# Turning round the gate/up product of the fuller expert of each pair in a one-core decoder step

## The reference, cut to what matters

```
D_MODEL, N_EXPERTS, TOP_K, EXPERT_DIM = 1024, 64, 8, 256
def one_block(args):
    tok_b, w_b, e = args
    xb = x_pad[tok_b]
    hb = jax.nn.silu(xb @ w_gate[e]) * (xb @ w_up[e])
    return (hb @ w_down[e]) * w_b[:, None]
...
return jax.ops.segment_sum(out.reshape(n_rows, d), tok_p, num_segments=t + 1)[:t]
```

## Time and profile before

| | |
|---|---|
| device time, median of three runs | 1811.39 us (1807.18 to 1811.45) |
| span of the profiled execution | 1803.0 us |
| before the expert stage (0 to 818.5 us) | 818.5 us |
| expert stage (818.5 to 1716 us) | 897.5 us, TensorE busy 893.16 us |
| after it (1716 to 1803 us) | 87.0 us |
| DMA share in the expert stage | 0.91 |

### The profile page before, as it was taken

How to read it: one execution, slowest core, us unless ns; L and a number is a source line. 1 busy time by engine, 2 the same in 40 slices (tenths; PEclk the granted TensorE clock), 3 DMA queues, 4 the chain that set the end, 5 groups by cost and what they waited for, 6 DMA issues and landing times.

```text
span 1803.0 us, 25610 instructions
## 1 busy us (share of the span) xinstructions
PE 1672.9 (93%) x8473; PEld 1204.3 (67%) x8474; DVE 1132.6 (63%) x1511; ACT 888.3 (49%) x1325; POOL 654.7 (36%) x555
## 2 busy tenths in 40 slices
PE   4999999589998898688999999999999999999997
PEld 3555555323356667366888888888888888888843
DVE  2355575541235556566777777777777777777746
ACT  1011111232336455136666776667676667676633
POOL 0056676300000000104555555555555555555410
PEclk8999999689999999789999999999999999999999
DMA  9688866677771113647998999989999989998874
GB/s 331 211 285 285 274 207 212 233 222 237 233 238 63 68 53 156 258 159 277 312 302 292 303 300 310 310 288 308 307 303 311 291 305 314 304 318 285 276 225 183
DMA packets 151909, 457.38 MB, mean 254 GB/s; under 512 B 29592, under 2 KB 39794, under 8 KB 126169
## 3 DMA queue, kind: packets, MB, share of 16 engines
q1 hardware_dynamic: 111097, 368.08, 55.7%
q0 software_dynamic: 30720, 69.83, 17.0%
q10 hardware_dynamic: 9960, 17.83, 2.9%
HBM read 403.40 MB, written 86.54 MB: 272 GB/s over the span
## 4 chain that ended last, share of the span: by engine, by line
PE 56%; DVE 2%; ACT 1%; issue 0%; DMA 0%; ACTq 0%; POOLq 0%; DVEq 0%
PE ps L2229 29%; PE ps L2246 15%; PE ps L2215 5%; PE ps L2534 2%; PE ps L2552 1%; PE ps L2253 1%; PE ps L1885 1%; PE ps L1856 1%; PE ps L1840 0%; DMA xg<-h_d,tokb 0%; DVE sums L1941 0%; DVE pairs L1908 0%; DVE gsc L1911 0%; ACT hT L2496 0%; DVE left L1931 0%
## 5 line engine op out<-in xcount | busy, mean ns | idle before, releaser
L2229 PE MATMUL ps<-hi_gu,xT_hi 128*128 128x512 f32 x768 | 309.5, 403 | 0.0
L2274 DVE TENSOR_TENSOR lo_gu<-raw_gu,hi_gu 128x1024 fp32r<-128x1024 f32 x256 | 304.3, 1221 | 4.5
L2229 PE MATMUL ps<-hi_gu,xT_lo 128*128 128x512 f32 x768 | 301.1, 392 | 0.0
L2229 PE MATMUL ps<-lo_gu,xT_hi 128*128 128x512 f32 x768 | 299.4, 390 | 0.0
L2168 ACT ACTIVATE hi_gu<-raw_gu 128x1024 fp32r<-128x1024 f32 x256 | 260.8, 1064 | 0.0
L2127 POOL DMA_INDIRECT acc_d<-yb,tokb x96 | 227.9, 2374 | 43.8 <-ACT yb L2182 24.9
L2108 POOL DMA_INDIRECT xg<-h_d,tokb x96 | 101.4, 1056 | 388.3 <-PE ps L2215 343.9
L602 PE MATMUL ps<-w_in_sb,hT 128*128 128x512 f32 x512 | 223.7, 594 | 1.1 <-ACT hT L466 1.1
L446 POOL TENSOR_TENSOR prod<-kring,qbc 128x512 f32<-128x512 f32 x128 | 158.8, 1270 | 177.1 <-DMA kring<-in_cache_k 119.2
L2182 ACT ACTIVATE yb<-ps,wslot 128x1024 f32<-128x1024 f32 x96 | 107.0, 1115 | 137.4 <-PE ps L2246 137.4
L602 PEld LDWEIGHTS ps<-w_in_sb,hT 128*128 128x128 f32 x512 | 95.9, 190 | 117.6 <-issue 116.3
(11 more groups left out here) (343 smaller groups left out, 2601.8 us busy)
## 6 DMA issues: line engine op xcount, KB each, us to landing
raw_gu<-in_expert_w_gate SPq DMA_DIRECT2D x64, 1024.0 KB, 8.6
raw_gu<-in_expert_w_up SPq DMA_DIRECT2D x64, 1024.0 KB, 12.1
raw_dn<-in_expert_w_down SPq DMA_DIRECT2D x64, 1024.0 KB, 7.6
kring<-in_cache_k SPq DMA_DIRECT2D x128, 256.0 KB, 3.2
vring<-in_cache_v SPq DMA_DIRECT2D x128, 256.0 KB, 3.1
adaw<-in_ada_w ACTq DMA_DIRECT2D x7, 2048.0 KB, 12.7
adaw<-in_ada_w SPq DMA_DIRECT2D x5, 2048.0 KB, 15.9
w_in_sb<-in_w_in SPq DMA_DIRECT2D x4, 2048.0 KB, 19.2
```

The costliest lines, as they stand in the source:

```text
L2229: last = pe.matmul(ps[:, 2 + b % 2, :].rearrange("p (a f) -> p a f", a=2), x[b % 2][:, k, :], w[:, :, k * F:(k + 1) * F], start=(k == 0 an ...
L2274: dve.tensor_tensor(lo_cut(n, u), raw_cut(n, u), hi_cut(n, u).bitcast(F32), ALU.subtract).then_inc(lo_made, 1)
```

## The change

The caps of the experts change. A table gives the heavy expert of pair p a cap of 224, 208, 192, 176 or 160 rows (4, 8, 8, 8 and 4 pairs; 192 on average) in place of 256; the light one stays at 128. With the counts above no expert is over its cap, before or after, so the overflow loop has no block in either.

For the heavy expert the operands of gate/up are turned round. The weights are stationary, 128 columns at a time, and the expert's transposed rows stream, all of them at once. They lie in `xT_h` as [chunk][hi | lo][cap], so that one matmul with w_hi streams both parts (2·cap columns: x_hi·w_hi into the first cap columns of a bank, x_lo·w_hi into the next), and a second one with w_lo streams x_hi (cap columns). The product is made in two halves of the hidden width, ch 0 and 1, each of 32 matmuls over both banks 2 and 3 (`gate_up_heavy`). Since the sum is in two halves of a bank, ScalarE copies the second half to SBUF (`second_halves`) and VectorE adds (`add_halves`) before silu. The hidden rows come out transposed, and the two blocks of the heavy expert need no `turn_h`. The down product of the light expert of the pair before stands between the two halves. The light expert is computed as before, from its own buffers, and its bank is one of the two.

The second block of a heavy expert gathers, evicts and scatters cap-128 rows in place of 128. The twelve cuts of a pair are spread over five places (`cuts_at`). The down weights are loaded with another split of the 256 hidden rows, so that a partition gets two pieces of 4 KB in place of one of 8 KB. The routing code computes the caps from the table.

```diff
+CAPS = [224] * 4 + [208] * 8 + [192] * 8 + [176] * 8 + [160] * 4 + [P] * PAIRS
...
-            w_from, = addressed(sp, ew_down[0][bass.ds(e, 1)].rearrange("o (p c) n -> p (o c n)", c=FC))
+            w_from, = addressed(sp, ew_down[0][bass.ds(e, 1)].rearrange("o (c p) n -> p (o c) n", p=P))
...
+                of = {HEAVY_FIRST: [(light, 0), (light, 1), (light, 2)],
+                      HEAVY_MID: [(light, 3), (heavy, 4)],
+                      HEAVY_LATE: [(heavy, 5), (light, 4)],
+                      LIGHT_FIRST: [(light, 5), (after, 0), (after, 1)],
+                      LIGHT_LATE: [(after, 2), (after, 3)]}[stage]
...
+            def second_halves(p, ch):
+                t, cap = 2 * p + ch, cap_of(2 * p)
+                act.wait_ge(gu_mm, turn_of(2 * p, ch))
...
+                act.activation(half2[:, :, 0:cap], ps[:, 2:4, cap:2 * cap], ACT.Copy).then_inc(half2_here, 1)
...
+            for p in range(PAIRS):
+                round_x(3 * p + 2)
+                round_weights(cuts_at(p, HEAVY_FIRST))
+                second_halves(p, 0)
+                gate_heavy(p, 0)
+                round_weights(cuts_at(p, HEAVY_MID))
+                if p:
+                    evict(3 * p - 1)
+                round_h_heavy(p, 0)
+                round_weights(cuts_at(p, HEAVY_LATE))
+                second_halves(p, 1)
+                gate_heavy(p, 1)
+                if p + 1 < PAIRS:
+                    round_x(3 * p + 3)
+                round_h_heavy(p, 1)
+                round_weights(cuts_at(p, LIGHT_FIRST))
+                gate_light(p)
+                if p + 1 < PAIRS:
+                    round_x(3 * p + 4)
+                round_weights(cuts_at(p, LIGHT_LATE))
+                evict(3 * p)
+                round_h_light(p)
+                evict(3 * p + 1)
...
+            def gate_up_heavy(p, ch):
+                n, cap = 2 * p, cap_of(2 * p)
+                x = xT_heavy(n)
+                pe.wait_ge(xT_made, 3 * p + 2)
+                if 2 * p + ch:
+                    pe.wait_ge(sums_h, 2 * p + ch)
+                for h, bank in enumerate((gate_bank(p), 5 - gate_bank(p))):
...
+                    for k in range(KC):
...
+                        cols = slice(k * F + ch * P, k * F + (ch + 1) * P)
+                        wh, wl = hi_gu[n % 2][:, h, cols], lo_gu[n % RAWS][:, h, cols]
...
+                            pe.matmul(ps[:, bank, 0:2 * cap], wh, x[:, k, :, :].rearrange("p a t -> p (a t)"),
+                                      start=(k == 0), stop=False)
+                            pe.matmul(ps[:, bank, 0:cap], wl, x[:, k, 0, :], start=False, stop=False)
...
+            def gate_up_light(p):
+                n = 2 * p + 1
+                pe.wait_ge(xT_made, 3 * p + 3)
+                pe.wait_ge(sums_h, 2 * p + 2)
...
             for p in range(PAIRS):
+                turn_x(3 * p + 2)
+                gate_up_heavy(p, 0)
+                if p:
+                    down(3 * p - 1)
+                gate_up_heavy(p, 1)
+                if p + 1 < PAIRS:
+                    turn_x(3 * p + 3)
+                gate_up_light(p)
+                if p + 1 < PAIRS:
+                    turn_x(3 * p + 4)
+                down(3 * p)
+                down(3 * p + 1)
+                turn_h(p)
...
+            def add_halves(p, ch):
+                cap = cap_of(2 * p)
+                dve.wait_ge(half2_here, 2 * p + ch + 1)
...
+                dve.tensor_tensor(gu_h[:, :, 0:cap], ps[:, 2:4, 0:cap], half2[:, :, 0:cap], ALU.add).then_inc(sums_h, 1)
```

More of the change, by code:

```diff
@@ L2023, in build @@
         yb = [place(f"yb{j}", 17 + 4 * j, [P, D]) for j in range(2)]
-        sg = [place(f"sg{j}", 33 + j, [P, F]) for j in range(2)]
-        hb = [place(f"hb{j}", 35 + j, [P, F]) for j in range(2)]
         hi_gu = [place(f"hi_gu{j}", 137 + 24 * j, [P, 2, KC * F], F32R) for j in range(2)]
@@ L2053, in expert_of, with cap_of, rows_of_block, turn_of @@
             return 2 * (b // 3) + (b % 3 == 2)
[L2055 to L2056 removed]
+        def cap_of(n):
+            return CAPS[n // 2] if n % 2 == 0 else P
+        def rows_of_block(b):
+            return cap_of(expert_of(b)) - P if b % 3 == 1 else P
         def last_block(n):
             return 3 * (n // 2) + 1 + n % 2
+        def turn_of(n, ch=1):
+            return 3 * (n // 2) + (3 if n % 2 else 1 + ch)
         GU_CUTS, CUTS = 4, 6
[L2063 to L2067 removed]
+        HEAVY_FIRST, HEAVY_MID, HEAVY_LATE, LIGHT_FIRST, LIGHT_LATE = range(5)
+        def cuts_at(p, stage):
+            heavy, light, after = 2 * p, 2 * p + 1, 2 * p + 2
+            of = {HEAVY_FIRST: [(light, 0), (light, 1), (light, 2)],
[3 more added lines that the diff above has]
+                  LIGHT_LATE: [(after, 2), (after, 3)]}[stage]
+            return [(n, u) for n, u in of if n < NE]
+        nth_cut = {}
+        for u in range(GU_CUTS):
+            nth_cut[0, u] = u + 1
+        for p in range(PAIRS):
+            for stage in range(5):
+                for cut in cuts_at(p, stage):
+                    nth_cut[cut] = len(nth_cut) + 1
+        assert len(nth_cut) == CUTS * NE
         def raw_cut(n, u):
@@ L2185, in experts_act @@
             round_x(0)
[L2186 to L2206 removed]
+            round_weights([(0, u) for u in range(GU_CUTS)])
@@ new lines, in gated, with rest_of_h_heavy @@
+            def gated(p, ch):
+                t, cap = 2 * p + ch, cap_of(2 * p)
+                gate, up = gu_h[:, gate_bank(p) - 2, 0:cap], gu_h[:, 3 - gate_bank(p), 0:cap]
+                dve.wait_ge(sgh_here, t + 1)
+                own(dve.tensor_tensor(gate, gate, sg_h[:, 0:cap], ALU.mult))
+                own.wait()
+                dve.tensor_tensor(gate, gate, up, ALU.mult).then_inc(gated_h, 1)
+            def rest_of_h_heavy(p, ch):
+                cap = cap_of(2 * p)
+                dve.wait_ge(hT_hi_made, turn_of(2 * p, ch))
+                dve.tensor_tensor(hT_h[:, ch, 1, 0:cap], gu_h[:, gate_bank(p) - 2, 0:cap], hT_h[:, ch, 0, 0:cap].bitcast(F32),
+                                  ALU.subtract).then_inc(hT_made, 1)
@@ new lines, in experts_dve @@
+            rest_of_x(0)
+            rest_of_weights([(0, u) for u in range(GU_CUTS)])
+            rest_of_x(1)
+            for p in range(PAIRS):
+                rest_of_x(3 * p + 2)
+                rest_of_weights(cuts_at(p, HEAVY_FIRST))
+                add_halves(p, 0)
+                gated(p, 0)
+                rest_of_weights(cuts_at(p, HEAVY_MID))
+                rest_of_h_heavy(p, 0)
+                rest_of_weights(cuts_at(p, HEAVY_LATE))
+                add_halves(p, 1)
+                gated(p, 1)
+                if p + 1 < PAIRS:
+                    rest_of_x(3 * p + 3)
+                rest_of_h_heavy(p, 1)
+                rest_of_weights(cuts_at(p, LIGHT_FIRST))
+                gated_light(p)
+                if p + 1 < PAIRS:
+                    rest_of_x(3 * p + 4)
+                rest_of_weights(cuts_at(p, LIGHT_LATE))
+                rest_of_h_light(p)
```

258 lines of the change are left out of this document (140 added, 118 removed).

## The result

The changed kernel takes 1833.76 us (median of 4 runs, 1821.52 to 1837.97), the kernel before, run beside it, 1809.29. The ratio is 1.0134, with a 95% interval of 1.0106 to 1.0162. The forecast was 1793, the range 1760 to 1830: the sign is wrong, and the range is missed by 4 us. The profiled execution took 1831.6 us, with a span of 1829.8.

A forecast was written before the change was run, and what follows sets the result against it. The expert stage was taken as TensorE's, 28.02 us a pair; a 27.1 us loop through three engines plus 0.3 of hand-overs gives 27.4, saving 19 us over 32 pairs, less 1 lost: 1793 us, range 1760 to 1830.

The forecast's parts named there:

- TensorE's work: Matmuls and transposes of a pair: 25.76 us against 28.02, alone giving back 2.26 us a pair, 72 in all.
- the price of 0.112: Heavy gate/up: each short matmul of 192 columns costs 0.112 us, set by the load of its stationary operand.
- The first rival: Heavy gate/up: short fp32r matmuls are dear, up to 0.33 us each, +178 us against the forecast, 1971; chance 0.13.
- The new wait for the sums: Before light gate/up: TensorE waits 1.35 us a pair until VectorE has added the halves of heavy half 1.
- that cover: Gather of a block: issued 12 us or more before its transposes, lands after 8.5, so costed at nothing.
- The DMA rival in its sharper form: evict(3p-1) waits for the scatter of block 3p-3; landing at 13 us gives 1837; chance of whole DMA rival 0.27.
- The first form of it: DMA engines loaded unevenly, up to 28.02 us a pair: pair stays at 28.0 and above, 1811 to 1820; whole rival 0.27.

The follow-up runs named there:

- the late load: Changed kernel with the load of the light expert's gate and up weights waiting for the transposes of the next heavy expert's first block: 1801.2 us.
- the order of the queue alone: Changed kernel with GpSimd issuing the gather of block 3p+3 ahead of the scatter of block 3p-3 instead of behind it: 1828.0 us.
- the cut alone: Changed kernel with one cut of light expert weights, (light, 4), moved out of the row ahead of the second sums: 1813.7 us.

## Why the prediction was wrong

- **TensorE's work**: right in the sum, by some luck in its parts. A long and a short matmul take 0.30 us, as forecast for a cap of 208, but split 0.20 and 0.10 and not 0.187 and 0.112: the price of 0.112, read from matmuls of 64 columns, is not what a short one costs here. The first rival is out.
- **The new wait for the sums**: right in place and size, but to be seen alone only in the run with the late load: 1.3 us, a period of 27.39 against the 27.4 of the forecast.
- **"By the same layout the gather of a block is issued 12 us or more before its transposes, and lands after 8.5. If that cover goes, TensorE waits for rows."** This is the step that failed. The lead was right: issued at 1009.30, needed at about 1021.6, 12.3 us. The landing was not: 13.1 us in the median of these blocks, and TensorE waited for rows 37.3 us between 900 and 1700. I took the median over all three kinds of block; for this kind it was 9.7 before already. And I looked at its lead alone and not at what is issued with it: now a scatter at 1007.38, and from 1008.3 to 1010.6 the 3 MB of weights that the end of the pair sets off. I had named just that burst, further down in the prediction, for the scatter. With the light expert's 2 MB out of the way the same gather lands after 10.9 us, and ahead of the scatter after 5.0.
- **The DMA rival in its sharper form**: right in mechanism (a landing holds evict(3p-1), 20 times from 900 to 1700 us), at a landing of 11.0 us in the median, where I thought that it decides from 11.6. A chance of 0.27 for it was low. That its 1837 is near the result is luck: it stood for a landing of 13 us of that scatter, and here the late rows and the clock made up the loss. The first form of it, engines full to 28 us, is out: with the same bytes a period of 26.8 is possible.
- **I priced the two as alternatives; they are in parallel**: each hides the other, which is why the order of the queue alone gave 0.3%, the cut alone 0.8%, and both 2.6%.
- **The clock had no term**, without a reason given. The forecast puts 1.35 us of idling into every pair and prices TensorE at full speed throughout. The half-level stretches cost 16 us, about as much as the late landings. Without them the time would be some 1818 us (an estimate, 1833.8 less 8 x 2.0), inside the range, but still slower than before.

The Trainium skill, "DMA: Bandwidth & Descriptors", Queues, rings and completion order, has the DMA engines serve their queues in turn, packet by packet. The landings agree with it in kind: the same gather takes 5.0 us when it is issued ahead of the scatter and the weights, and 13.1 behind the one and beside the other. How much of that is due to the turns isn't shown.

## What to carry to other kernels

Where a change moves work within a loop, list for every transfer the moment of issue and what else is issued in the same few microseconds, and take the landing of that very transfer, not the median over its line. When an edit that removes the largest wait gains nothing, look for a second one of the same length before blaming bandwidth; try both edits together. Idle time of a microsecond or two in every round also has to be charged with the clock.

## What the runs showed of the hardware

- The half level (1.2 GHz) came without any long idle: in the 8 periods that had such a stretch TensorE had waited 1.8 to 3.0 us in all, around the transposes ahead of the light gate/up. In the 23 others it waited 0.5 to 2.3 us (the first pair apart), so the two overlap, and just what tips it isn't shown by these runs. A period with a stretch is 2.0 us longer; the stretch itself, 3.41 us at half speed, accounts for 1.7 of it.
- A gather of 128 rows of 4 KB lands after 4.3 us at the least and 14.1 at the most (blocks 3p+3 with the queue's new order, and in the changed kernel), by what is issued ahead of it and beside it.
- A matmul that streams 208 fp32r columns behind a new stationary operand of 128 columns costs 0.10 us, in turn with long ones of 416 columns at 0.20. As few columns as that are not dear.
- Halving the size of the pieces of a 1 MB load (8 to 4 KB) cost nothing here, at 297 to 300 GB/s from 900 to 1700 us.
